# First gates and weight loads regrouped, and the attention bias added by VectorE instead of TensorE, in a hybrid decoder layer on eight cores

## The chip, the cores and the metric

The kernel runs on one Trainium2 chip, on all 8 of its cores. Each core works on one sequence of the batch and talks to no other. The time is the device time of the slowest core in microseconds (us), the median of several runs; lower is better. TensorE is called PE in the rows, VectorE DVE, ScalarE ACT, GpSimd POOL, and SP is the engine that issues most DMAs.

## What is computed

One decoder layer for x of 8 x 4096 x 1024, with two token mixers whose results are gated and merged, and an MLP:

```python
h = rmsnorm(x, norm1_w)
q, k, v, xr, yr, ga, gr = split(h @ w_in)          # 512, 512, 512, 1024 x4
# A: block-sparse attention, 8 heads of 64; q and k normed per head
s = (q @ k.T) * scale + bias_tab[bucket(q_pos - k_pos)]   # 32 buckets per head
# a query sees its own block of 256 keys (causal) and the 3 past blocks whose
# mean key scores best
A = softmax(s) @ v
# B: causal conv of width 4, then the gated linear recurrence
u = conv(xr);  a = exp(-8 * sigmoid(u @ Wa) * softplus(-lam))
hr = scan(a, sqrt(1 - a*a) * sigmoid(u @ Wi) * u)
B = hr * gelu(yr)
merged = sigmoid(ga) * (A @ w_proj_attn) + sigmoid(gr) * (B @ w_proj_rnn)
x = x + merged @ w_out
x = x + relu(rmsnorm(x) @ w_ff1)**2 @ w_ff2
```

## The kernel before

The program is recorded as a list of operations, and a list scheduler with a cost model of its own turns the list into one fixed order per engine. Each engine then works through its order and waits on semaphores. The order in which the code records work therefore sets priorities, and the scheduler may pull a later piece forward. Every engine instruction carries the line of the recorder (L475) and every DMA that of the DMA recorder (L480), so rows are told apart by their tile names.

The work of one core falls into three stages.

**Stage A, the front end.** The 4096 tokens are 32 tiles of 128. For a tile, `FEn` loads x (`xs`), norms it (`hb`, needing the norm weights `nw`), transposes it on PE and copies it to `hT`, which is also stored to `h_s` in HBM. `FEp` makes q and k and normalizes them per head, with short POOL, ACT and DVE steps (`ssq`, `qa`, `ktm`), and `FEv` makes v: 24 matmuls of 512 columns with `wqkv` per tile. Between the tiles the code records the recurrence of the first chunk: a chunk is 512 tokens, `RNN(0, ct)` stands at tiles 14, 16, ..., 28 for the eight column tiles ct, and `RNN2(0, g)` at tiles 21 and 29. `RNN` is 16 matmuls (`wx`, `wy`) and the convolution on DVE (`cv`), `RNN2` the two gates, the scan on DVE (`ii`) and the product `orn`.

**Stage B.** For chunks s = 1 to 7 the code records `RNN(s)`, `GATE1(s-1, m)` for the eight m, and `RNN2(s)`. `GATE1(c, m)` is 8 matmuls with `wga` (their tanh `t1` is stored to HBM as `t_s`), 8 with `wgr`, and 8 with `wpr` on `orn`; DVE multiplies the last two (`t2`, stored as `rm_s`).

**Stage C.** Attention for chunks c = 0 to 7 is cut into small units that are dealt out between dense units (gating, output projection, `W1`, `W2`) by a running `goal` and by `marks`, before which a chunk's attention must be recorded. During attention(0) the dense units are `GATE1(7, m)`. A unit of attention is one key tile of 128 keys of one head: a score matmul S into a PSUM bank (`qT`, `kTr`; banks 0 and 1, and bank 3 once `GATE1(7)` is done), the bias for the tiles that need one, an exp on ACT (`PT`) and up to four matmuls with V into an output bank (`Vr`). After the last tile of a head DVE takes a reciprocal (`rcp`) and scales the output (`otm`). The bias is a matmul of the identity with a table `BT`, added to the score bank; it covers 128 columns for the tile just before the chunk and 256, 256, 256 and 128 for the chunk's own four tiles. Gating loads `t1r` and `rmr` from HBM and combines them on DVE into `mT`.

Of the kernel before, what the change touches and what calls it, by code (L numbers as in the profile page):

```python
# [1297 lines left out]
```

How the kernel before makes its waits and increments, by code:

```python
        def run(ename, h):  # L282
            for i in order[ename]:
                for s, v in waits[i]:
                    h.wait_ge(sems[s], v)
                ins = ops[i].fn(h)
                if sig[i] is not None:
                    ins.then_inc(sems[sig[i][0]], 16 if ops[i].dsem is not None else 1)
            if ename == "sync":
                for s, v in fw.items():
                    h.wait_ge(sems[s], v)
```

## Time and profile before

| what | value |
| --- | --- |
| median of 3 runs | 2408.96 us (2406.88 to 2409.96) |
| the profiled execution, its own time | 2405.57 us |
| span of its slowest core, core 5 | 2404.0 us (the others 2392.4 to 2401.3) |
| PE busy | 2288.5 us, 95% |
| ACT busy | 1321.6 us, 55% |
| DVE busy | 1070.9 us, 45% |
| POOL busy | 612.6 us, 25% |
| mean granted TensorE clock, by core | 0.983 to 0.988 of full speed |

All rows are from the slowest core of that execution. Busy shares are averages over the three stages: the front end runs from 0 to about 210 us, stage B to about 830 us (the first score matmul starts at 832.6), and the rest is stage C. "PEclk" is the clock that was granted to TensorE as a share of full speed, so a stretch can lose time with PE idle or with PE slow.

### The profile page before, as it was taken

Reading aid. Unit: us, or ns where it says so; the run is one execution under the profiler, and the core shown is the slowest. Engines: PE = TensorE matmul, PEld = TensorE weight load, DVE = VectorE, ACT = ScalarE, POOL = GpSimd, SP = SyncE. Lnnn points to the kernel's source line nnn. Section 1 sums busy time; section 2 is a strip of 40 time slices with the busy share of each in tenths; the row PEclk is TensorE's granted clock in tenths of the full one; section 3 lists DMA queues with packets and bytes.
Section 4 is the critical chain, followed back from the end, with each engine's and each line's share of the span. In section 5 each row is a group of like instructions: output and inputs, shape, how many; then the busy total and the mean of one; then the engine's idle time right before and its main releaser. Section 6 shows DMA issues by size and latency. Waiting matters only on the chain.

```text
span 2404.0 us, 43880 instructions; the slowest of 8 cores (2392.4 to 2404.0 us)
## 1 busy us (share of the span) xinstructions
PE 2288.5 (95%) x14806; PEld 1127.5 (47%) x14806; DVE 1070.9 (45%) x1913; ACT 1321.6 (55%) x2341; POOL 612.6 (25%) x593
## 2 busy tenths in 40 slices
PE   3899989999999988999999999999999999999999
PEld 1444434444444444454555545555555455554444
DVE  2478777778778732423333332314222321232332
ACT  2568666676776735554636537554665375563111
POOL 3587753444444401101101001101100200110200
PEclk9899999999999988999999999999999999999999
DMA  6963665556562458256555565556455644644543
GB/s 148 236 192 135 147 141 117 114 121 143 123 136 72 126 168 238 96 167 168 166 166 165 181 162 182 144 172 192 139 169 169 189 142 152 178 159 135 173 166 123
DMA packets 194598, 373.47 MB, mean 155 GB/s; under 512 B 15507, under 2 KB 106684, under 8 KB 176316
## 3 DMA queue, kind: packets, MB, share of 16 engines
q1 hardware_dynamic: 188684, 336.04, 45.3%
q0 software_dynamic: 5696, 34.61, 9.5%
q8 instruction: 126, 2.06, 0.4%
q14 instruction: 92, 0.75, 0.1%
HBM read 332.30 MB, written 91.76 MB: 176 GB/s over the span
## 4 chain that ended last, share of the span: by engine, by line
PE 83%; DMA 5%; issue 4%; DVE 3%; POOL 2%; ACT 1%; SPq 1%; DVEq 0%; POOLq 0%; ACTq 0%
PE bank L475 83%; POOL s_ssq L475 2%; DMA s_xs<-x 1%; DMA s_t1r<-t_s 1%; DMA s_rmr<-rm_s 1%; SPq L480 1%; DMA k_s<-s_kst 1%; DMA rm_s<-s_t_0 1%; DMA s_wpr<-wpr_p 0%; DMA s_qT<-s_mskT 0%; DVE s_cv L475 0%; DVE s_ii L475 0%; DVE s_ssq L475 0%; DVE s_mT L475 0%; ACT L475 0%
## 5 line engine op out<-in xcount | busy, mean ns | idle before, releaser
L475 ACT ACTIVATE s_PT<-bank 128x512 bf16<-128x512 f32 (+3 forms) x1152 | 588.7, 564 | 315.1 <-PE bank L475 308.2
L475 PE MATMUL bank<-s_h2T,s_wsl 128*128 128x512 bf16 x2048 | 522.6, 380 | 3.2 <-DVE s_h2T L475 2.9
L475 PE MATMUL bank<-s_uT,s_wsl 128*128 128x512 bf16 x2048 | 513.0, 379 | 0.0
L475 PEld LDWEIGHTS bank<-s_Vr,s_PT 128*128 128x128 bf16 x4224 | 272.0, 98 | 257.0 <-issue 25.8
L475 PE MATMUL bank<-s_qT,s_kTr 80*128 80x512 bf16 (+3 forms) x1152 | 370.6, 364 | 4.9 <-DMA s_qT<-s_mskT 3.6
L475 ACT ACTIVATE s_rl<-bank 128x512 f32<-128x512 f32 x256 | 152.8, 597 | 320.3 <-PE bank L475 311.0
L475 PE MATMUL bank<-s_Vr,s_PT 128*128 128x65 bf16 x4224 | 314.0, 194 | 9.1 <-ACT s_PT L475 7.3
L475 DVE TENSOR_TENSOR s_uT<-s_rl 128x512 bf16<-128x512 f32 x176 | 122.6, 697 | 378.9 <-ACT s_rl L475 378.8
L475 PEld LDWEIGHTS bank<-s_h2T,s_wsl 128*128 128x128 bf16 x2048 | 189.4, 98 | 178.8 <-issue 7.7
L475 PEld LDWEIGHTS bank<-s_uT,s_wsl 128*128 128x128 bf16 x2048 | 182.5, 98 | 163.5 <-issue 2.9
L475 DVE TENSOR_TENSOR s_x1T<-bank,s_x1T 128x512 f32<-128x512 f32 x128 | 88.2, 689 | 365.2 <-PE bank L475 364.8
L475 POOL TENSOR_TENSOR s_uT<-s_rl 128x512 bf16<-128x512 f32 x80 | 83.9, 1048 | 608.6 <-ACT s_rl L475 559.9
L475 PE MATMUL bank<-s_wqkv,s_hT 128*128 128x512 bf16 x768 | 193.6, 396 | 13.5 <-ACT s_hT L475 9.0
L475 DVE SCALAR_TENSOR_TENSOR s_cv<-s_xr,s_pvec,s_cv 128x512 f32<-128x512 f32 x192 | 160.6, 896 | 1.0 <-ACT s_cv L475 0.3
L475 POOL TENSOR_TENSOR s_mT<-s_t1r,s_rmr 128x512 bf16<-128x512 f32 x32 | 40.8, 1274 | 440.9 <-DVE s_t1r L475 413.3
L475 PE MATMUL bank<-s_mT,s_wo 128*128 128x512 bf16 x512 | 131.2, 388 | 10.4 <-DVE s_mT L475 6.0
L475 POOL TENSOR_TENSOR s_orn<-s_ii,s_gq 128x512 bf16<-128x512 f32 x64 | 113.1, 1780 | 105.5 <-DVE s_ii L475 105.4
L475 POOL TENSOR_TENSOR s_ss<-s_ss,s_sqt 128x512 f32<-128x512 f32 x48 | 60.8, 1267 | 290.9 <-ACT s_sqt L475 289.7
L475 PEld LDWEIGHTS bank<-s_qT,s_kTr 80*128 80x128 bf16 x1152 | 108.8, 98 | 54.4 <-issue 8.6
L475 PE MATMUL bank<-s_orn,s_wpr 128*128 128x512 bf16 x512 | 125.1, 385 | 5.9 <-POOL s_orn L475 4.1
L475 PE MATMUL bank<-s_hTb,s_wga 128*128 128x512 bf16 x512 | 123.4, 382 | 5.3 <-ACT s_cv L475 5.3
L475 PE MATMUL bank<-s_hTb,s_wy 128*128 128x512 bf16 x512 | 122.7, 382 | 2.3 <-ACT s_gq L475 2.3
(120 smaller groups left out, 2728.8 us busy)
## 6 DMA issues: line engine op xcount, KB each, us to landing
s_wsl<-wff_s SPq DMA_DIRECT2D x128, 1024.0 KB, 6.0
s_xs<-x SPq DMA_DIRECT2D x32, 512.0 KB, 4.8
wff_s<-wff_p POOLq DMA_DIRECT2D x16, 1024.0 KB, 13.5
s_t1r<-t_s SPq DMA_DIRECT2D x64, 256.0 KB, 3.7
s_rmr<-rm_s SPq DMA_DIRECT2D x64, 256.0 KB, 4.3
s_x1T<-xT SPq DMA_DIRECT2D x64, 256.0 KB, 4.3
outT<-s_x1T SPq DMA_DIRECT2D x64, 256.0 KB, 5.3
h_s<-s_hT SPq DMA_DIRECT2D x32, 256.0 KB, 4.4
```

What stands on the lines that cost most here:

```text
L475: return P.add(eng, lambda e, m=meth, kw=kw: getattr(e, m)(**kw), reads, writes, cost=c_, lat=lat, fam=fam, tag=tag or (writes[0] if write ...
L480: return P.add(q, lambda e: e.dma_start(out=out, in_=in_), reads, writes, dsem=dsem, cost=(1000.0 if q == "gpsimd" else 80.0), nbytes=nb, ...
```

## The change

It has five parts. First, the bias is no longer a matmul: after S, DVE adds `BT` to the bank in place. Second, `GATE1` is cut in two: `GA(s, m)` with `wga` is recorded with chunk s itself, from s = 0 on, and `GR(s-1, m)` with `wgr` and `wpr` a chunk later, so that only `GR(7, m)` is left for attention(0). Third, `RNN(0)` and `RNN2(0)` leave the front end: column tiles 0 to 3 stand at tiles 28 to 31, the rest in `stageB(0)`. Fourth, the first loads stand in another order and wait for one another, `xs` has 4 buffers and `hT` 6, and the weights of the recurrence are loaded at every second tile. Fifth, `wpa` and `wo` are loaded before attention(0) instead of during it, for which SBUF is laid out anew.

```diff
         load_x(0)
+        dma("sync", nw, nw_d, "c0b", [], ["nw"])
         dma("sync", identb, cid_d, "c0a", [], ["identb"])
-        dma("sync", nw, nw_d, "c0b", [], ["nw"])
-        load_x(1)
...
-        load_x(2)
...
+        for t in range(1, NXS):
+            load_x(t, P.after("nw") if t == 1 else P.after("xs%d" % (t - 1)))
...
-            if wB:
+            if t % 2 == 0 and wB:
                 w_, src, nm = wB.pop(0)
...
-            if t >= 14 and t % 2 == 0 and t < 30:
-                RNN(0, [(t - 14) // 2], rbank)
-            if t == 21:
-                RNN2(0, 0, rbank)
-            if t == 29:
-                RNN2(0, 1, rbank)
+            if t >= 28:
+                RNN(0, [t - 28], rbank)
...
-        def GATE1(c, m, bank):
-            hk = ["hTb%d" % (c % NHB)]
+        def GA(c, m, bank):
...
+            for dt_ in range(8):
+                op("tensor", "matmul", ["hTb%d" % (c % NHB), "wga%d" % p], ["B%d" % b], tag="gate", out=bankf[b], lhsT=wga[p][:, dt_, o_:o_ + 128], rhs=h_[:, :, dt_, :],
+                   start=(dt_ == 0), stop=(dt_ == 7))
+            op("scalar", "activation", ["B%d" % b, "hbias"], ["t1_%d" % s], out=t1[s], in_=bankf[b], func=AF.Tanh, scale=0.5, bias=hbias[:, m, 2:3])
+            dma("sync", t1_s[c, m], t1[s], "t1_%d" % s, ["t1_%d" % s], ["t1_s%d_%d" % (c, m)])
+
+        def GR(c, m, bank):
...
         def stageB(s, g, between=None):
-            RNN(s, range(NR * g, NR * g + NR), dbank)
+            if s + g > 0:
+                RNN(s, range(NR * g, NR * g + NR), dbank)
...
+            for half in range(2):
+                for m in range(4 * g + 2 * half, 4 * g + 2 * half + 2):
+                    GA(s, m, dbank)
+                    if s > 0:
+                        GR(s - 1, m, dbank)
+                if half == 0:
+                    if between is not None:
+                        between()
+                    RNN2(s, g, dbank)
...
-        for s in range(1, NCH):
+        for s in range(NCH):
...
-                           lhsT=kTr[ks][0:80, hi * nk * 128 + kt * 128:hi * nk * 128 + (kt + 1) * 128], rhs=qT[s][0:80, h, q0:CH], start=True, stop=bias is None)
+                           lhsT=kTr[ks][0:80, hi * nk * 128 + kt * 128:hi * nk * 128 + (kt + 1) * 128], rhs=qT[s][0:80, h, q0:CH], start=True, stop=True)
                         if bias is not None:
                             qb, b0, nb_ = bias
-                            op("tensor", "matmul", ["BT", "identb"], ["B%d" % sb], tag="S", out=bankf[sb][:, qb - q0:qb - q0 + nb_], lhsT=identb,
-                               rhs=BT[:, h, b0:b0 + nb_], start=False, stop=True)
+                            sl_ = bankf[sb][:, qb - q0:qb - q0 + nb_]
+                            op("vector", "tensor_tensor", ["B%d" % sb, "BT"], ["B%d" % sb], tag="bias", out=sl_, in0=sl_, in1=BT[:, h, b0:b0 + nb_], op=ALU.add)
...
         def early():
+            dma("sync", wpa, wpo[:, 0:4, :], "wpa", ["wpo_s0"], ["wpa"])
+            for i in range(2):
+                dma("sync", wo[:, 4 * i:4 * i + 4, :], wpo[:, 4 + 4 * i:8 + 4 * i, :], "wo", ["wpo_s1"], ["wo:%d" % i])
...
-                GATE1(NCH - 1, m, gbank7)
...
+                GR(NCH - 1, m, gbank7)
...
-        extend([(5200.0, gate1u(m)) for m in range(8)])
...
+        for m in range(8):
+            extend([(3460.0, gate1u(m))])
+            if m == 5:
+                marks[0] = len(dense)
+            if m > 5:
+                extend(g0[2 * m - 12:2 * m - 10])
```

What the scheduler makes of it is seen in each engine's order. The first place is the start of SP's order, with the loads of x (`xs`), the norm weights (`nw`) and the small constants; first before, then after the change, with the semaphores waited for.

```order
L480 DMA s_xs0<-x 128x1024
L480 DMA s_identb<-c_identb 128x128
L480 DMA s_nw<-nw_bc 128x1024
L480 DMA s_xs1<-x 128x1024
L480 DMA s_xs2<-x 128x1024
L480 DMA s_pvec<-pvec 128x88
```

```order
L480 DMA s_xs0<-x 128x1024
L480 DMA s_nw<-nw_bc 128x1024
L480 DMA s_identb<-c_identb 128x128
L480 DMA s_qkcol<-qk_col 128x2
L480 DMA s_pvec<-pvec 128x88
L480 DMA s_nwc<-nw_col 128x8
L480 DMA s_mtab<-c_mtab 128x768
L480 DMA s_cv0<-c_G 33x384
L480 DMA s_ii0<-rel_bias 32x8 [waits e_vector]
L480 DMA s_xs1<-x 128x1024 [waits d_c0b]
```

The second x tile (`xs1`) has moved from the fourth place to the tenth, behind all the constants, and waits for `nw` (semaphore c0b) to land.

The second place is PE's order near the end of attention(0), whose heads have four key tiles (S of 512, 384, 256 and 128 columns). `s_hTb,s_wgr` and `s_orn,s_wpr` are what is left of the gates, `s_Vr,s_PT` the matmuls with V. First before, from the last pieces of the gates on:

```order
L475 MATMUL bank<-s_hTb,s_wgr 128x512
L475 MATMUL bank<-s_orn,s_wpr 128x512 x8
L475 MATMUL bank<-s_qT,s_kTr 128x256
L475 MATMUL bank<-s_BT,s_identb 128x256
L475 MATMUL bank<-s_Vr,s_PT 128x65
L475 MATMUL bank<-s_qT,s_kTr 128x384
L475 MATMUL bank<-s_BT,s_identb 128x256
L475 MATMUL bank<-s_Vr,s_PT 128x65 x4
```

And after:

```order
L475 MATMUL bank<-s_orn,s_wpr 128x512
L475 MATMUL bank<-s_Vr,s_PT 128x65
L475 MATMUL bank<-s_kmBD,s_qp 128x32 x4
L475 MATMUL bank<-s_identb,s_maskb 128x128
L475 MATMUL bank<-s_kmBD,s_qp 128x32 x4
L475 MATMUL bank<-s_identb,s_maskb 128x128
L475 MATMUL bank<-s_qT,s_kTr 128x512
L475 MATMUL bank<-s_identb,s_maskb 128x128
L475 MATMUL bank<-s_Vr,s_PT 128x65 x4
L475 MATMUL bank<-s_qT,s_kTr 128x256
L475 MATMUL bank<-s_qT,s_kTr 128x384
```

Before, the last gate matmuls stand ahead of the last two heads; now they stand ahead of the last four, and behind them PE has only scores and V matmuls until the transposes at the end of attention(0). One gate unit is left for attention(1).

The third place is DVE's order at the start of attention(1), with gating(0) beside it; bank0 and bank1 are score banks, `d_t1r0` and `d_rmr1` wait for DMAs. Before:

```order
L475 SCALAR_TENSOR_TENSOR s_t1r0<-s_t1r0,bank5 128x512 [waits e_tensor,d_t1r0]
L475 SCALAR_TENSOR_TENSOR s_t1r1<-s_t1r1,bank6 128x512 [waits e_tensor,d_t1r1]
L475 TENSOR_TENSOR s_mT<-s_t1r1,s_rmr1 128x512 [waits e_vector,d_rmr1]
L475 RECIPROCAL s_rcp<-bank2 128x4 [waits e_tensor]
L475 TENSOR_TENSOR s_otm<-bank2,s_rcp 128x4x64 [waits e_vector]
L475 SCALAR_TENSOR_TENSOR s_t1r0<-s_t1r0,bank7 128x512 [waits d_t1r0]
```

And after:

```order
L475 SCALAR_TENSOR_TENSOR s_t1r0<-s_t1r0,bank5 128x512 [waits e_tensor,d_t1r0]
L475 TENSOR_TENSOR bank1<-bank1,s_BT 128x128 [waits e_tensor]
L475 SCALAR_TENSOR_TENSOR s_t1r1<-s_t1r1,bank6 128x512 [waits e_tensor,d_t1r1]
L475 TENSOR_TENSOR bank0<-bank0,s_BT 128x256 [waits e_tensor]
L475 TENSOR_TENSOR s_mT<-s_t1r1,s_rmr1 128x512 [waits e_vector,d_rmr1]
L475 TENSOR_TENSOR bank1<-bank1,s_BT 128x256 [waits e_tensor]
L475 TENSOR_TENSOR bank0<-bank0,s_BT 128x256 [waits e_tensor]
L475 TENSOR_TENSOR bank1<-bank1,s_BT 128x128 [waits e_tensor]
```

The five adds of a head now stand among gating's instructions on the same engine, some right behind one that waits for a load.

## Rows read from the trace of the kernel before

**Rows 1.** Page, busy time by engine (PE matmuls, PEld weight loads).

```profile
PE 2288.5 (95%) x14806; PEld 1127.5 (47%) x14806; DVE 1070.9 (45%) x1913; ACT 1321.6 (55%) x2341; POOL 612.6 (25%) x593
```

**Rows 2.** Windows: length, busy us (instructions) per engine, PEclk, DMA share, GB/s.

```profile
0.00:60.00 60.00, 23.09 (x110) 10.18 (x111) 16.53 (x39) 16.52 (x27) 22.33 (x32) 0.93 0.62 147
60.00:120.00 60.00, 52.40 (x285) 25.00 (x284) 28.44 (x42) 32.94 (x53) 31.04 (x41) 0.87 0.92 236
120.00:340.00 220.00, 199.26 (x1157) 97.55 (x1155) 172.84 (x270) 146.53 (x232) 157.63 (x179) 0.98 0.59 158
340.00:840.00 500.00, 494.13 (x2277) 222.45 (x2276) 383.33 (x540) 350.06 (x529) 211.69 (x180) 1.00 0.52 119
840.00:900.00 60.00, 52.14 (x335) 26.79 (x334) 21.23 (x63) 21.42 (x46) 4.71 (x3) 0.90 0.50 168
900.00:950.00 50.00, 38.72 (x347) 19.98 (x346) 12.85 (x28) 29.06 (x63) 5.05 (x4) 0.88 1.01 270
950.00:1120.00 170.00, 159.77 (x1117) 80.28 (x1115) 64.22 (x183) 80.62 (x155) 26.21 (x23) 0.95 0.48 142
1120.00:2340.00 1220.00, 1208.40 (x8912) 617.94 (x8910) 356.95 (x732) 634.88 (x1223) 148.77 (x129) 1.00 0.54 164
2340.00:2404.00 64.00, 60.61 (x281) 27.30 (x279) 14.52 (x21) 9.55 (x16) 5.20 (x5) 0.99 0.36 132
```

**Rows 3.** Timeline of PE in attention beside the MLP: start, us, instruction, count.

```profile
1608.73 0.60 PE L475 MATMUL bank<-s_qT,s_kTr 80*128 80x512 bf16 x2
1609.16 0.22 PE L475 MATMUL bank<-s_BT,s_identb 128*128 128x128 bf16 x1
1609.22 0.38 PE L475 MATMUL bank<-s_qT,s_kTr 80*128 80x512 bf16 x1
1609.44 0.27 PE L475 MATMUL bank<-s_BT,s_identb 128*128 128x256 bf16 x1
1609.55 1.02 PE L475 MATMUL bank<-s_uT,s_wsl 128*128 128x512 bf16 x4
```

**Rows 4.** Groups by form on PE: busy us, mean ns | idle before, releaser.

```profile
L475 PE MATMUL bank<-s_BT,s_identb 128*128 128x256 bf16 x192 | 51.3, 274 | 0.0
L475 PE MATMUL bank<-s_BT,s_identb 128*128 128x128 bf16 x120 | 26.5, 222 | 0.0
```

**Rows 5.** Groups by form on DVE, 900 to 2340 us, same columns.

```profile
L475 DVE SCALAR_TENSOR_TENSOR s_t1r<-s_t1r,bank 128x512 f32<-128x512 f32 x64 | 43.8, 685 | 66.3 <-PE bank L475 46.4 <-DMA s_t1r<-t_s 18.8
...
L475 DVE TENSOR_TENSOR s_otm<-bank,s_rcp 128x256 bf16<-128x256 f32 x56 | 23.7, 424 | 5.3
...
L475 DVE TENSOR_TENSOR s_gm<-bank,s_mtab 128x128 f32<-128x128 f32 x24 | 6.8, 283 | 0.4 <-PE bank L475 0.3
```

**Rows 6.** Timeline of the start, all engines; in brackets the idle before.

```profile
16.73 1.28 DVE L475 SCALAR_TENSOR_TENSOR s_hb<-s_xs,s_rstd,s_nw 128x1024 bf16<-128x1024 f32 x1 [14.88 <-DMA s_nw<-nw_bc]
...
24.70 1.06 ACT L475 ACTIVATE s_junk<-s_xs 128x1024 bf16<-128x1024 f32 x1 [17.54 <-DMA s_xs<-x]
...
26.99 3.57 PE L475 MATMUL bank<-s_wqkv,s_hT 128*128 128x512 bf16 x8 [7.71 <-ACT s_hT L475]
...
36.88 4.36 PE L475 MATMUL bank<-s_wqkv,s_hT 128*128 128x512 bf16 x10
```

**Rows 7.** Chain that ended last, 0 to 340 us: start, us, what.

```profile
73.71 15.45 DMA k_s<-s_kst
```

**Rows 8.** Waits of PE, 200 to 345 us: us in total, times, longest.

```profile
PE bank L475 <- ACT s_cv L475: 5.3, 1, 5.3
PE bank L475 <- ACT s_hT L475: 3.9, 1, 3.9
```

**Rows 9.** Timeline of DVE at the end of attention(0), two heads' ends.

```profile
892.63 0.18 DVE L475 RECIPROCAL s_rcp<-bank 128x4 f32<-128x4 f32 x1 [1.02 <-PE bank L475]
...
895.10 0.18 DVE L475 RECIPROCAL s_rcp<-bank 128x4 f32<-128x4 f32 x1 [1.75 <-PE bank L475]
```

**Rows 10.** Waits of DVE, 840 to 960 us: us in total, times, longest.

```profile
DVE s_t1r L475 <- DMA s_t1r<-t_s: 12.9, 5, 4.1
```

More of the change, by code:

```diff
@@ L539, in build_nc @@
         pA_peak = cur[0]
+        orn, wga, wgr, wpr = [], [], [], []
         tok_tiles = x_d.rearrange("(n p) d -> n p d", p=128)
@@ L778, in build_nc @@
         st.append(contextlib.ExitStack())
-        for i in range(2, NHB):
-            hTb[i] = alloc("hTb%d" % i, [TPC, 8, 128], BF16)
-        wga, wgr, wpr = [], [], []
+        orn += [alloc("orn%d" % i, [CH], BF16) for i in range(8)]
+        baseC = cur[0]
+        hTb[2] = alloc("hTb2", [TPC, 8, 128], BF16)
         for p in range(4):
@@ L798, in GATE1 @@
             sos = [(c * 8 + i) % NORN for i in range(8)]
-            for j, (w_, wk, dst, dk) in enumerate(((wga[p], "wga%d" % p, t1[s], "t1_%d" % s), (wgr[p], "wgr%d" % p, t2[s], "t2_%d" % s))):
-                b = bank()
-                for dt_ in range(8):
-                    op("tensor", "matmul", hk + [wk], ["B%d" % b], tag="gate", out=bankf[b], lhsT=w_[:, dt_, o_:o_ + 128], rhs=h_[:, :, dt_, :],
-                       start=(dt_ == 0), stop=(dt_ == 7))
-                op("scalar", "activation", ["B%d" % b, "hbias"], [dk], out=dst, in_=bankf[b], func=AF.Tanh, scale=0.5, bias=hbias[:, m, 2 + j:3 + j])
-            dma("sync", t1_s[c, m], t1[s], "t1_%d" % s, ["t1_%d" % s], ["t1_s%d_%d" % (c, m)])
+            b = bank()
+            for dt_ in range(8):
+                op("tensor", "matmul", ["hTb%d" % (c % NHB), "wgr%d" % p], ["B%d" % b], tag="gate", out=bankf[b], lhsT=wgr[p][:, dt_, o_:o_ + 128], rhs=h_[:, :, dt_, :],
+                   start=(dt_ == 0), stop=(dt_ == 7))
+            op("scalar", "activation", ["B%d" % b, "hbias"], ["t2_%d" % s], out=t2[s], in_=bankf[b], func=AF.Tanh, scale=0.5, bias=hbias[:, m, 3:4])
             b = bank()
@@ L822, in build_nc @@
             dma("gpsimd", wga[p], wr_d[2, p].rearrange("p (a b) -> p a b", a=8), "wga%d" % p, [], ["wga%d" % p])
+        for p in range(4):
             dma("gpsimd", wgr[p], wr_d[3, p].rearrange("p (a b) -> p a b", a=8), "wgr%d" % p, [], ["wgr%d" % p])
@@ L856, in build_nc @@
         st.append(contextlib.ExitStack())
-        kTr = [alloc("kTr%d" % i, [S], BF16) for i in range(2)]
-        qT = [alloc("qT%d" % i, [NH, CH], BF16) for i in range(2)]
-        qp = alloc("qp", [4, CH], BF16)
+        kTr = [alloc("kTr0", [S], BF16)]
+        wpa = alloc("wpa", [4, D], BF16)
+        wo = alloc("wo", [8, D], BF16)
+        sqt = [alloc("sqt%d" % i, [CH], F32) for i in range(2)]
         alloc("gap", [16], F32)
-        Vr = [alloc("Vr%d" % i, [NCH * VW], BF16) for i in range(2)]
+        qT = [alloc("qT0", [NH, CH], BF16)]
+        Vr = [alloc("Vr0", [NCH * VW], BF16)]
         gm = alloc("gm", [NH, 16], F32)
@@ L869, in build_nc @@
         rcp = alloc("rcp", [4], F32)
-        otm = alloc("otm", [4, 512], BF16)
         assert cur[0] <= endX, (cur[0], endX)
+        kTr.append(alloc("kTr1", [S], BF16))
+        qT.append(alloc("qT1", [NH, CH], BF16))
+        qp = alloc("qp", [4, CH], BF16)
+        Vr.append(alloc("Vr1", [NCH * VW], BF16))
         NPT = 6
         PT = [alloc("PT%d" % i, [CH], BF16) for i in range(NPT)]
-        oT = [alloc("oT%d" % i, [4, CH], BF16) for i in range(2)]
-        wpa = alloc("wpa", [4, D], BF16)
-        wo = alloc("wo", [8, D], BF16)
-        t1r = [alloc("t1r%d" % i, [CH], F32) for i in range(2)]
+        otm = alloc("otm", [4, 512], BF16)
+        oT = [alloc("oT0", [4, CH], BF16)]
+        ss = alloc("ss", [CH], F32)
+        rs2 = alloc("rs2", [CH], F32)
+        t1r = [alloc("t1r0", [CH], F32)]
+        assert cur[0] <= endR, (cur[0], endR)
+        if endR - cur[0] > 64:
+            alloc("gap2", [(endR - cur[0]) // 64 * 32], BF16)
+        mT = alloc("mT", [8, CH], BF16)
+        oT.append(alloc("oT1", [4, CH], BF16))
+        NRL = 2
+        rl = [alloc("rl%d" % i, [CH], F32) for i in range(NRL)]
+        t1r.append(alloc("t1r1", [CH], F32))
         rmr = [alloc("rmr%d" % i, [CH], F32) for i in range(2)]
+        assert cur[0] <= baseC, (cur[0], baseC)
         uT = alloc("uT", [16, CH], BF16)
```

69 lines of the change are left out of this document (29 added, 40 removed).

## Prediction

> **What bounds the kernel now.** I read the busy times first: TensorE is busy for 95% of the span, no other engine for more than 55% [rows 1]. So the questions are where matmul time goes away and where TensorE idles or runs slow. The windows answer the second: of each stretch take the length less the PE busy time, and add the length times what PEclk lacks of 1. From 0 to 60 us that is 36.9 idle + 4.2 of clock, 60 to 120: 7.6 + 7.8, 120 to 340: 20.7 + 4.4, so 82 us lost before 340. Stage B, 340 to 840, loses 5.9 in all. From 840 to 1120, with attention(0), attention(1) and the first gating and MLP, it is 7.9 + 6.0, 11.3 + 6.0 and 10.2 + 8.5, so 50 us. From 1120 to 2340 TensorE loses 11.6 us of 1220 [rows 2]. The kernel is thus TensorE-bound where most of the attention runs, and has two weak places, the start and the hand-over to attention, which the regrouping touches.
>
> **The bias.** The identity matmuls last 274 and 222 ns in the groups [rows 4], but the engine pipelines, so the price is the spacing of starts: the 128-column one starts at 1609.16 and the next matmul at 1609.22, 0.06 us; the 256-column one holds 1609.44 to 1609.55, 0.11 us [rows 3]. All 192 and 120 of them make 192 x 0.11 + 120 x 0.06 = 28.3 us. They are worth this only where TensorE is the bound. Chunks 2 to 7 lie there: 48 heads of three 256s and two 128s, 48 x (0.33 + 0.12) = 21.6 us. Attention(0) and (1) run where TensorE idles, and I count nothing for them. **Term: -21.6**, bounds -28.3 and, were the slots idle, 0.
>
> The 128-column price can be set against a page. The row says 0.06 us. The Trainium skill, "TensorE: Matmul & The Clock Gate", section "Back-to-back issue gap", gives a sustained spacing of about 81 ns for 128 columns; by it the 120 narrow ones would be worth 9.7 us instead of 7.2, and the sum would be 2.5 us lower. The row is of this very matmul, so I keep it.
>
> On VectorE the trace has no such add. The nearest rows with one PSUM operand: `otm` with 256 columns 424 ns, `gm` with 128 columns and a float result 283 ns [rows 5]. That is 192 x 0.424 + 120 x 0.283 = 115 us more on an engine that is busy 357 of 1220 us in the long stretch [rows 2], so its own time is covered by matmuls. What can be exposed is latency: S, add, exp and the V matmuls of a tile follow one another, and the score bank is held 0.3 to 0.4 us longer. With dense matmuls as filler this costs little: the exp already stands in that chain, and the 11.6 us lost in the stretch are all that it and everything else cost. Bounds: 0 (all covered) and 115 (each add exposed). It is nearest to the covered row, so I take **+3**.
>
> **The start.** Now the first `hb` waits 14.9 us for `nw` and begins at 16.73; the second x tile lands at 24.70, when ACT begins on it [rows 6]. After the change `nw` is second and comes sooner, but x1 leaves only once `nw` is there and still shares the DMA engines with `wqkv`, so tile 1 will hardly be earlier than 24. What can be gained is that q, k and v of tile 0 run in between: its first 8 matmuls start at 26.99, the next ones only at 36.88 [rows 6]. As DVE and POOL are what the front end's later tiles wait for, I take -3 (bounds 0 and -12, the gap between those two blocks plus what `nw` brings).
>
> **Front end and first stage of B.** Without the weights of the recurrence at every tile and with RNN(0) later, DMA is less crowded between 40 and 120 us: it is 92% busy there, and the chain has one link of 15.45 us, a store of k [rows 2, 7]. I take -8 (bounds 0 and -15.4, all that 60 to 120 loses). Against this stands that nothing is saved on DVE: RNN(0) takes as much wherever it stands. Stage B spends 383 of 500 us on DVE [rows 2]; a chunk there has 336 matmuls of 512 columns at 0.215 us (two S take 1608.73 to 1609.16 [rows 3]), 72 us, and so 55 us of DVE. The new stage 0 has some 230 matmuls, 50 us, for the same 55 us: DVE becomes its limit, for about 5 us. The hand-over now has waits of 5.3 and 3.9 us [rows 8], which GA(0) can fill as it needs no recurrence. I take -4 for this part, stall included (bounds +5 and -9.2). **Term for 0 to 340: -15**, bounds +5 and -37.
>
> **Hand-over to attention.** GA(7), 64 matmuls of 0.215 = 13.8 us, moves from attention(0) into stage B. That is no gain in itself: matmuls are moved, and attention(0) loses their cover. By the order, four heads instead of two now run bare. A bare head takes 895.10 - 892.63 = 2.5 us from one reciprocal to the next [rows 9], of which S, bias and V matmuls fill about 1; with four adds of 0.28 to 0.42 over two banks I make it 3.3, idle 2.4. So 4 x 2.4 - 2 x 1.5 = +6.6. In attention(1) the adds lengthen a head's chain by about as much as the matmuls shorten TensorE's list, +1. In return the two `wo` loads and the `wpa` load are out of the way when DMA is at 1.01 [rows 2], and DVE's 12.9 us of waiting for `t1r` [rows 10] should shrink; I take -8 from a bound of -12.9. The last gates beside gating(0) fill a bubble, -4. That sums to -4.4. **Term: -4**, bounds +10 and -15.
>
> **Sum:** -21.6 + 3 - 15 - 4 = -37.6. On the profiled execution's 2405.6 this gives 2368.0. The median stands 3.4 above that execution, so I forecast **2371 us**, 1.6% faster. That, give or take 15, is the first case: 2356 to 2385.
>
> **Rivals.** *A, VectorE's line becomes the bound (slower).* The adds stand in DVE's fixed order between instructions that wait: 18.8 us for `t1r` [rows 5], most of it in attention(1) [rows 10], and the new order puts adds right behind those. While one waits, the add, the exp and the V matmuls wait too, and TensorE behind them. For: the order itself, and a whole-chain exposure of 115 us. Against: in the long stretch DVE is 29% busy, and with the adds about 37%. It decides from the point where some 38 us more than my 3 are exposed, a third of 115. At half of the 115, 57 us, the time is 2409 - 38 + 54 = 2425. The Trainium skill, "PSUM — Partial Sum Buffer", section "Engine vs sequencer instructions", says that VectorE's queue is strictly first in, first out, so nothing overtakes the waiting instruction; no row yet shows adds behind one.
>
> *B, the regrouping gives nothing.* The front end is held by short DVE and POOL steps, which stay, DVE takes over stage 0, and the barer heads eat what the DMAs give. Only the bias remains: 2409 - 21.6 + 3 = 2390, range 2385 to 2404. For: DVE at 79% and POOL at 72% from 120 to 340 [rows 2].
>
> *C, all of it pays.* Both weak places reach near their lower bounds, -30 and -12: 2409 - 21.6 - 42 = 2345, range 2325 to 2355. For: the 82 and 50 us lost there. Against: the regrouping leaves the longest DVE and POOL chains as they are.
>
> *D, the freed slots are idle slots.* If TensorE merely waits elsewhere once the bias matmuls are gone and the regrouping nets nothing, the time stays at 2409. Against: the identity matmuls start right on the spacing of their neighbours [rows 3], with no idle before them [rows 4].
>
> **How the numbers follow.** First case 0.50, B 0.22, C 0.11, D 0.06, A 0.11. The prediction is the first. Range 2336 to 2404: it reaches through B above and into most of C below, leaving out A, D and the low end of C, about 0.2. A measurement of this kernel can tell about 0.2% from no change, 5 us. Faster by more: first, B and C, 0.83. Same: D, 0.06. Slower: A, 0.11.
>
> **What would show it.** Right: no identity matmuls with `BT` on PE, and 312 adds near 424 and 283 ns on DVE; 1120 to 2340's work some 21 us shorter with PE still near 99% busy; the start to the first gates of stage B about 15 us shorter; `t1r` waits below 12.9. Wrong: PE waits for `PT` that were not there, growing in step with DVE's waits on DMA or on PE; adds far from 0.4 us; a front end as long as before; bare heads of attention(0) well over 3.3 us; or a lower granted clock where heads run bare, which would cost again as much as the idling.

## The result and the profile after

The changed kernel takes 2395.51 us in the median (2392.58 for its profiled execution, the lowest of its runs), against 2409.46 for the kernel before on the same chip. The ratio is 0.994, with a 95% interval of 0.992 to 0.9959: faster by 0.6%, where 1.6% was forecast. In the profiled execution of one experiment below (e1) one die was disturbed, so its rows are from a core of the other die.

The busy times by engine [rows 1 before]:

```profile
PE 2267.0 (95%) x14494; PEld 1105.3 (46%) x14494; DVE 1171.3 (49%) x2225; ACT 1333.0 (56%) x2345; POOL 612.7 (26%) x593
```

312 matmuls are gone from PE, and 312 instructions have come to DVE. The adds, in the groups by form, are close to the rows that priced them [rows 5]:

```profile
L475 DVE TENSOR_TENSOR bank<-bank,s_BT 128x256 f32<-128x256 f32 x192 | 79.3, 428 | 74.9 <-PE bank L475 73.8
L475 DVE TENSOR_TENSOR bank<-bank,s_BT 128x128 f32<-128x128 f32 x120 | 35.5, 296 | 76.0 <-PE bank L475 75.9
```

The windows of the same stretches, of core 6, the slowest [rows 2]:

```profile
0.00:60.00 60.00, 17.62 (x63) 7.02 (x64) 9.26 (x28) 11.92 (x19) 11.89 (x20) 0.91 0.61 140
60.00:120.00 60.00, 53.22 (x311) 26.84 (x310) 37.46 (x54) 36.24 (x60) 40.44 (x56) 0.90 0.82 222
120.00:340.00 220.00, 207.00 (x1202) 101.65 (x1201) 159.20 (x245) 150.49 (x233) 150.74 (x171) 0.99 0.66 173
340.00:840.00 500.00, 490.02 (x2255) 220.07 (x2253) 385.84 (x547) 347.00 (x524) 212.47 (x180) 1.00 0.53 118
840.00:900.00 60.00, 45.20 (x249) 20.99 (x247) 35.95 (x94) 24.06 (x46) 11.38 (x8) 0.85 0.45 134
900.00:950.00 50.00, 38.37 (x270) 18.45 (x270) 24.64 (x65) 25.49 (x54) 3.80 (x3) 0.70 0.80 230
1120.00:2340.00 1220.00, 1209.88 (x8835) 610.58 (x8834) 422.85 (x938) 647.21 (x1239) 151.97 (x131) 1.00 0.54 166
```

The long stretch is as full as before (1209.88 of 1220 busy) although DVE has 66 us more to do in it. The front end from 60 to 340 is fuller, the first 60 us are emptier, and the hand-over from 840 to 950 is worse, in idle time and in granted clock.

Windows at fixed times hold different work in the two kernels. Milestones do not. The groups by tile show the first and the last start of an instruction (count, shortest/median/longest ns, first to last start us); the first score matmul (`s_kTr`) ends stage B, and the first matmul on `s_h2T` starts the first MLP. Before:

```profile
L475 PE MATMUL bank<-s_qT,s_kTr x1152: 219/380/631, 832.6 to 2194.8; 80*128 80x512 bf16 x175, 80*128 80x256 bf16 x11, 80*128 80x384 bf16 x4, 80*128 80x128 bf16 x2
L475 PE MATMUL bank<-s_h2T,s_wsl x2048: 376/379/634, 971.7 to 2372.6; 128*128 128x512 bf16 x187
```

After:

```profile
L475 PE MATMUL bank<-s_qT,s_kTr x1152: 217/380/631, 845.6 to 2179.1; 80*128 80x512 bf16 x172, 80*128 80x256 bf16 x13, 80*128 80x384 bf16 x5, 80*128 80x128 bf16 x2
L475 PE MATMUL bank<-s_h2T,s_wsl x2048: 376/379/634, 981.0 to 2359.4; 128*128 128x512 bf16 x187
```

GA(7), 64 matmuls, now lies before the first of these milestones. The table takes it out of either side at the 13.8 us of the prediction:

| stretch | before | after | moved by GA(7) | difference | forecast |
| --- | --- | --- | --- | --- | --- |
| start to first score | 832.6 | 845.6 | -13.8 | -0.8 | -15 |
| first score to first `h2T` | 139.1 | 135.4 | +13.8 | +10.1 | -4 |
| first to last `h2T` | 1400.9 | 1378.4 | 0 | -22.5 | -21.6 + 3 |
| last `h2T` to the end of the span | 31.4 | 31.3 | 0 | -0.1 | 0 |

They add up to the 13.3 us between the spans. The bias did what was forecast, and a little more. Both terms of the regrouping missed, by 14 us each.

Two cautions. The table is of the slowest core of each run, and the cores of one run differ: the second stretch takes 134.9 to 141.0 us on the eight cores before and 131.3 to 137.2 after. The medians of the eight cores give much the same differences, -2.5, +10.3 and -24.9. And the 13.8 us assume that GA(7) costs its full length in either place. The run e9 below shows that it does not, so of the first two rows only their sum is firm: +9.3, where -19 was forecast.

### The profile page after: what moved, and what is told of

Same layout as the page of the kernel before. It is cut to its first block, busy times and chain, and to the rows that moved or that the text cites. A ratio compares the mean times of both kernels' runs of the same rounds, so it can differ in the third digit from the quotient of the medians.

```text
span 2390.7 us, 43783 instructions; the slowest of 8 cores (2374.7 to 2390.7 us)
## 1 busy us (share of the span) xinstructions
PE 2267.0 (95%) x14494; PEld 1105.3 (46%) x14494; DVE 1171.3 (49%) x2225; ACT 1333.0 (56%) x2345; POOL 612.7 (26%) x593
## 3 DMA queue, kind: packets, MB, share of 16 engines
q0 software_dynamic: 5696, 34.61, 10.1%
## 4 chain that ended last, share of the span: by engine, by line
PE 84%; DMA 5%; issue 4%; DVE 3%; POOL 2%; ACT 1%; SPq 0%; DVEq 0%; POOLq 0%; ACTq 0%
PE bank L475 84%; POOL s_ssq L475 1%; DMA s_pvec<-pvec 1%; DMA s_t1r<-t_s 1%; DMA s_xs<-x 1%; DMA rm_s<-s_t_0 1%; DMA s_qT<-s_mskT 1%; DMA outT<-s_x1T 1%; DVE s_cv L475 0%; SPq L480 0%; DVE s_ii L475 0%; DMA s_x1T<-xT 0%; ACT s_PT L475 0%; DVE s_ssq L475 0%; DVE s_t1r L475 0%
## 5 line engine op out<-in xcount | busy, mean ns | idle before, releaser
L475 PE MATMUL bank<-s_uT,s_wsl 128*128 128x512 bf16 x2048 | 518.9, 379 | 1.5 <-DVE s_mskT L475 0.9
L475 PE MATMUL bank<-s_h2T,s_wsl 128*128 128x512 bf16 x2048 | 516.8, 380 | 0.8 <-DVE s_h2T L475 0.8
L475 PE MATMUL bank<-s_qT,s_kTr 80*128 80x512 bf16 (+3 forms) x1152 | 376.0, 370 | 9.2 <-ACT s_PT L475 4.0
L475 PE MATMUL bank<-s_Vr,s_PT 128*128 128x65 bf16 x4224 | 315.5, 195 | 12.1 <-ACT s_PT L475 11.7
L475 PE MATMUL bank<-s_wqkv,s_hT 128*128 128x512 bf16 x768 | 191.5, 396 | 21.2 <-ACT s_hT L475 16.4
L475 DVE TENSOR_TENSOR bank<-bank,s_BT 128x256 f32<-128x256 f32 (+1 forms) x312 | 111.3, 378 | 150.9 <-PE bank L475 149.7
L475 PEld LDWEIGHTS bank<-s_qT,s_kTr 80*128 80x128 bf16 x1152 | 108.7, 99 | 54.9 <-issue 16.5
L475 PE MATMUL bank<-s_hTb,s_wgr 128*128 128x512 bf16 x512 | 124.2, 383 | 3.5 <-ACT s_t_0 L475 2.0
```

What stands on the lines that cost most here:

```text
L475: return P.add(eng, lambda e, m=meth, kw=kw: getattr(e, m)(**kw), reads, writes, cost=c_, lat=lat, fam=fam, tag=tag or (writes[0] if write ...
```

## The experiments

Each time is given as a ratio to the kernel before, run beside it on the same chip (its 95% interval in brackets). The changed kernel was run again, on the chip of e15, e11 and e6, and gave 0.993 (0.9917 to 0.9944); with the first 0.994 that makes two marks to compare with. Ratios from different chips are compared with more care.

> The changed kernel once more, beside the next three on one chip: 0.992 to 0.996 of the kernel before.

**The parts apart.** The first run puts the identity matmul back into the changed kernel, the second puts the add alone into the kernel before.

```diff
 # e1_matmul_bias, on the changed kernel
-                            op("vector", "tensor_tensor", ["B%d" % sb, "BT"], ["B%d" % sb], tag="bias", out=sl_, in0=sl_, in1=BT[:, h, b0:b0 + nb_], op=ALU.add)
+                            op("tensor", "matmul", ["BT", "identb"], ["B%d" % sb], tag="S", out=bankf[sb][:, qb - q0:qb - q0 + nb_], lhsT=identb,
+                               rhs=BT[:, h, b0:b0 + nb_], start=False, stop=True)
...
 # e2_add_alone, on the kernel before: the same lines with + and - exchanged
```

> The changed kernel with the bias as identity matmuls again: the regrouping alone. Theory T1 (the adds save 21 us where TensorE is the bound and cost some 10 in attention(0) and attention(1); the regrouping nets about nothing because its start is later): 2403 to 2411 us. Rival T2 (the regrouping gains the forecast 15 to 20 us and the adds give nothing back): 2388 to 2395 us.

> The kernel before with the bias added by VectorE, nothing regrouped. T1: 2409 - 21, plus 1.4 us for each of two bare heads of attention(0) and about 4 us in attention(1), so 2391 to 2397 us. T2 (the adds' latency eats what the matmuls free): 2405 us or more.

Measured: the regrouping alone 1.0003 (0.9982 to 1.0023), the add alone 0.9913 (0.9889 to 0.9937). T1 holds: the whole gain is the bias, and the regrouping is worth nothing (e2 came out some 3 us faster than T1's 2391 to 2397). The milestones say the same: with the add alone the scores start at 838.8, `h2T` at 982.3, and it ends at 2363.4, so 143.5 and 1381.1 us against 139.1 and 1400.9.

```profile
L475 PE MATMUL bank<-s_qT,s_kTr x1152: 217/380/634, 838.8 to 2183.0; 80*128 80x512 bf16 x172, 80*128 80x256 bf16 x12, 80*128 80x384 bf16 x4, 80*128 80x128 bf16 x4
L475 PE MATMUL bank<-s_h2T,s_wsl x2048: 376/379/634, 982.3 to 2363.4; 128*128 128x512 bf16 x187
```

For the regrouping alone, on core 3, the hand-over takes 976.4 - 843.8 = 132.6 us and the long stretch 1396.9:

```profile
L475 PE MATMUL bank<-s_qT,s_kTr x1152: 216/379/631, 843.8 to 2194.7; 80*128 80x512 bf16 x172, 80*128 80x256 bf16 x13, 80*128 80x384 bf16 x4, 80*128 80x128 bf16 x3
L475 PE MATMUL bank<-s_h2T,s_wsl x2048: 376/379/634, 976.4 to 2373.3; 128*128 128x512 bf16 x187
```

So on these cores the add costs the hand-over 4.4 us (143.5 - 139.1), the regrouping 7.3 (132.6 + 13.8 - 139.1), and together they make 11.7, near the 10.1 measured. By the medians of the cores (for e1 of cores 0 to 3) it is 2.1 and 5.7, so the split holds to about 2 us. The 7.3 rests on the 13.8 us of GA(7).

**The start.** The timeline of the changed kernel shows two things that the prediction did not see:

```profile
8.92 1.28 DVE L475 SCALAR_TENSOR_TENSOR s_hb<-s_xs,s_rstd,s_nw 128x1024 bf16<-128x1024 f32 x1 [7.07 <-POOL s_rstd L475]
16.38 1.01 PE L475 MATMUL bank<-s_identb,s_hb 128*128 128x128 bf16 x8 [16.38 <-DMA s_identb<-c_identb]
...
28.86 0.22 ACT L475 ACTIVATE s_tmp<-s_pvec 128x8 f32<-128x8 f32 x1 [21.25 <-DMA s_pvec<-pvec]
...
29.29 0.99 ACT L475 COPY s_hT<-bank 128x1024 bf16<-128x1024 bf16 x1
...
30.53 3.57 PE L475 MATMUL bank<-s_wqkv,s_hT 128*128 128x512 bf16 x8 [13.15 <-ACT s_hT L475]
```

`hb` is ready at 10.2, 8 us sooner than before [rows 6], but the identity, now behind `nw`, lands at 16.4; and the copy of `hT`, ready from 17.4, runs at 29.29, because on ACT it stands behind an exp of `pvec`, which waits 21.25 us for its load. The code records that exp at tile 6; the scheduler hoisted it to the place right behind the first tile's square.

The kernel before has the same fault in a milder form. Its first copy stands on ACT behind the square of the second x tile, the row at 24.70 of [rows 6], which waits for that tile to land:

```profile
25.75 0.99 ACT L475 COPY s_hT<-bank 128x1024 bf16<-128x1024 bf16 x1
```

```diff
 # e15_pvec_late
-                dma("sync", pvec, pvec_d.rearrange("p (t j) -> p t j", t=8, j=11), "c0c", [], ["pvec"])
+                dma("sync", pvec, pvec_d.rearrange("p (t j) -> p t j", t=8, j=11), "c0c", [], ["pvec"], extra=P.after("hT%d" % (5 % NHT)))
 # e5_start: the same, and
+        dma("sync", identb, cid_d, "c0a", [], ["identb"])
         dma("sync", nw, nw_d, "c0b", [], ["nw"])
-        dma("sync", identb, cid_d, "c0a", [], ["identb"])
 # e17_unchained: e15_pvec_late, and
-            load_x(t, P.after("nw") if t == 1 else P.after("xs%d" % (t - 1)))
+            load_x(t)
```

> The changed kernel with the identity loaded ahead of nw again and the load of pvec held back until the sixth tile has been transposed. T1 (the first copy of hT stands behind an exp that waits for pvec until 28.9 us, and the first transpose waits for the identity until 16.4): the first q matmul starts near 22 instead of 30.5 and 6 to 11 us are gained, 2384 to 2390 us. Rival (wqkv or the second x tile sets the time, or stage 0 gives it back): 2393 to 2398 us.

> The changed kernel with one edit: the load of pvec waits for the sixth tile's hT, nw stays ahead of the identity. T1 (the exp that waits for pvec in ACT's line is what holds the first tile; the identity's place does not matter, since wqkv lands only near 21 us): the first q matmul near 21 us instead of 30.5, and as much gained as with the identity ahead too, 0.6 to 0.9% under the changed kernel. Rival (the identity's wait is half of it): under 0.4%.

> pvec late as in e15_pvec_late, and the first x loads no longer wait for one another or for nw. If the chaining delays the second tile for nothing: x1 lands before 28 us instead of 31.6 and 2 to 5 us are gained on e15_pvec_late. If the chaining protects wqkv and the identity: the first transpose comes after 18 us, and it is 0 to 4 us slower.

Measured: e5_start 0.9868 (0.9838 to 0.9898), e15_pvec_late 0.9886 (0.9868 to 0.9904), e17_unchained 0.9855 (0.9834 to 0.9876). Holding `pvec` back, that one edit, gains 0.44% on the changed kernel beside it, 10.6 us. That lies between T1's 0.6 to 0.9% and the rival's 0.4%. The copy no longer waits, as T1 says, and the first q matmul starts at 18.65, sooner than the 21 expected:

```profile
16.28 1.01 PE L475 MATMUL bank<-s_identb,s_hb 128*128 128x128 bf16 x8 [16.28 <-DMA s_identb<-c_identb]
17.39 1.01 ACT L475 COPY s_hT<-bank 128x1024 bf16<-128x1024 bf16 x1 [9.54 <-PE bank L475]
...
18.65 3.57 PE L475 MATMUL bank<-s_wqkv,s_hT 128*128 128x512 bf16 x8 [1.35 <-ACT s_hT L475]
```

The identity still lands at 16.3. With it ahead as well (e5_start) the ratio is 0.18% lower, on another chip and with overlapping intervals, so what its place is worth can't be told. As a whole e5_start gained 0.6 to 0.7%, 15 to 17 us, more than its T1 had. The chaining of the x loads may cost something: with it the second tile's square starts at 31.57, without it at 23.77, and the ratio goes from 0.9886 to 0.9855. The intervals overlap, and the two were on different chips, so that step, some 7 us, is likely rather than shown.

e17_unchained also warns against reading too much into the first q matmul. There the copy stands behind the square of the second tile again, and the first q matmul starts at 26.07, as late as in the kernel before:

```profile
23.77 1.06 ACT L475 ACTIVATE s_junk<-s_xs 128x1024 bf16<-128x1024 f32 x1 [16.67 <-DMA s_xs<-x]
24.83 0.99 ACT L475 COPY s_hT<-bank 128x1024 bf16<-128x1024 bf16 x1
26.07 2.72 PE L475 MATMUL bank<-s_wqkv,s_hT 128*128 128x512 bf16 x6 [9.11 <-ACT s_hT L475]
```

Yet by the windows TensorE is busy for 29.45 of the first 60 us, against 25.51 in e15_pvec_late and 17.62 in the changed kernel. So the load of `pvec` is what cost the time, but a first matmul that starts soon is not what the gain follows: what the first 60 us get done is nearer to it.

**Where the front end's gain goes.** The changed kernel's front end is faster once it runs: its last matmul with `wqkv` starts at 276.5 instead of 321.9 (not at about 210, as the section on the profile before has it), without RNN(0). But from there to the 64th `wpr` matmul, near 400, the windows show TensorE idling again:

```profile
84.00:276.00 192.00, 183.96 (x1153) 94.14 (x1151) 138.56 (x219) 118.90 (x191) 142.75 (x172) 0.99 0.74 200
276.00:400.00 124.00, 113.91 (x520) 50.08 (x519) 88.67 (x130) 97.34 (x143) 57.77 (x51) 0.99 0.39 99
```

10 of 124 us are idle where before it was 2.1 of 65 (62.90 busy from 322 to 387). DVE is busy 88.67 of 124, 72%, so it is not the limit that the prediction named.

```diff
 # e16_rnn0_early
-            if t >= 28:
-                RNN(0, [t - 28], rbank)
+            if t >= 22 and t % 2 == 0 and t < 30:
+                RNN(0, [(t - 22) // 2], rbank)
```

> The changed kernel with the first four column tiles of RNN(0) recorded at tiles 22, 24, 26 and 28 instead of 28 to 31. If stage 0 loses its 12 us because the recurrence of chunk 0 starts too late: 3 to 8 us gained, the front end ending a little later and the first wpr matmuls earlier. If the chain of the recurrence itself holds stage 0 (DVE and ACT steps in turn), or the front end gives it back: within 3 us of the changed kernel.

Measured 0.9939 (0.9917 to 0.996), no change: the recurrence's late start is not the cause. That its chain of DVE and ACT steps holds stage 0 fits, but is argued, not shown.

**The hand-over.** Where the bare heads run, the reciprocals of DVE stand 3.9 us apart, against 2.5 before [rows 9] and 3.3 forecast:

```profile
895.95 0.17 DVE L475 RECIPROCAL s_rcp<-bank 128x4 f32<-128x4 f32 x1
...
899.87 0.17 DVE L475 RECIPROCAL s_rcp<-bank 128x4 f32<-128x4 f32 x1
```

Not all of this is the add. With the regrouping alone (e1, core 3), where the bias is a matmul, the bare heads stand 3.2 us apart:

```profile
898.07 0.18 DVE L475 RECIPROCAL s_rcp<-bank 128x4 f32<-128x4 f32 x1 [2.48 <-PE bank L475]
...
901.25 0.18 DVE L475 RECIPROCAL s_rcp<-bank 128x4 f32<-128x4 f32 x1 [2.47 <-PE bank L475]
```

What the add does there shows in TensorE's waits for the exp (`PT`), 840 to 960 us, in this order: before, after, the regrouping alone (e1, core 3), the add alone (e2).

```profile
PE bank L475 <- ACT s_PT L475: 4.5, 12, 0.7
PE bank L475 <- ACT s_PT L475: 12.3, 23, 1.3
PE bank L475 <- ACT s_PT L475: 5.0, 14, 0.5
PE bank L475 <- ACT s_PT L475: 13.7, 22, 1.8
```

These waits are one of the signs by which the prediction said it would be wrong, and they come with the add alone.

The granted clock is lower too: from 900 to 950 PEclk is 0.70, where it was 0.88. Over the whole of 840 to 1120, before and after:

```profile
840.00:1120.00 280.00, 250.63 (x1795) 127.05 (x1794) 98.30 (x274) 131.09 (x263) 35.98 (x30) 0.93 0.58 170
```

```profile
840.00:1120.00 280.00, 241.80 (x1617) 117.81 (x1616) 145.02 (x400) 132.99 (x260) 41.00 (x34) 0.88 0.56 164
```

Idle rises from 29.4 to 38.2 us, the clock's share from 0.07 x 280 = 19.6 to 0.12 x 280 = 33.6. The clock's share counts idle time as well, in which a low clock costs nothing, so it is an upper bound. Which runs have the lower clock is clear. Those that keep identity matmuls in chunks 0 and 1 (before, e1, e3, e6, e18, e20) have 0.92 or 0.93 in this window, those that have none there (after, e2, e7, e8, e9, e11, e15, e16, e17) 0.86 to 0.90. What it costs is not: e7, without any bias, has 0.88 as well, and its hand-over is among the shortest.

DVE's waits for `t1r`, 12.9 us before [rows 10], have all but gone after the change. It was not the moved loads that did it. In order: after, the regrouping alone (e1, core 3), the add alone (e2).

```profile
DVE s_t1r L475 <- DMA s_t1r<-t_s: 1.1, 2, 0.6
DVE s_t1r L475 <- DMA s_t1r<-t_s: 13.5, 4, 6.9
DVE s_t1r L475 <- DMA s_t1r<-t_s: 2.6, 2, 1.4
```

With `wo` and `wpa` loaded early and no adds, DVE waits as long as before; with the adds and those loads where they were, it hardly waits. All eight cores of e2 say the same (at most 2.8 us). So the wait shrank with the adds, not with the loads. That DVE has the adds to do while the data comes in fits this, and then the shorter wait is no gain.

Four edits take the hand-over apart. The first keeps matmuls for the chunks of the hand-over, the second leaves the bias out, the third keeps GA(7) as filler in attention(0), the fourth deals attention(0) out over all eight gate units and records gating(0) behind it.

```diff
 # e3_matmul_first_two: identity matmul if c < 2, else the add
+                        if bias is not None and (c < 2):
...
+                        elif bias is not None:
 # e7_no_bias: neither
 # e9_ga7_filler
-                    GA(s, m, dbank)
+                    if s < NCH - 1:
+                        GA(s, m, dbank)
...
+                GA(NCH - 1, m, gbank7)
                 GR(NCH - 1, m, gbank7)
...
-            extend([(3460.0, gate1u(m))])
+            extend([(5200.0, gate1u(m))])
 # e11_pace
-            if m == 5:
-                marks[0] = len(dense)
-            if m > 5:
-                extend(g0[2 * m - 12:2 * m - 10])
-        extend(g0[4:5])
+        marks[0] = len(dense)
+        extend(g0[0:5])
...
-            goal = tot0 * (i + 1) / 6 if i < 5 else ...
+            goal = tot0 * (i + 1) / 9 if i < 8 else ...
```

> The changed kernel with identity matmuls for chunks 0 and 1 only, adds for chunks 2 to 7. T1 (in the bare heads the add lengthens the chain from 2.5 to 3.9 us a head): 8 to 12 us under the changed kernel, 2384 to 2388 us. Rival (the hand-over is slow for lack of filler alone, the add does not matter): 2394 to 2398 us.

> The changed kernel with no bias at all, neither matmul nor add (the scores lack it). What it is faster than the changed kernel by is all that the 312 adds cost. T1 (the adds are covered from chunk 2 on and cost in the hand-over, mostly by TensorE's lower clock): 8 to 14 us under the changed kernel, nearly all of it between 840 and 960 us. Rival (they cost everywhere, in step with their number): over 20 us, spread over the long stretch. Third way (the bare heads cost the same without them): under 4 us.

> The changed kernel with GA(7) kept out of stage B and done with GR(7) during attention(0), 64 matmuls of filler more there. If missing filler is what the hand-over lost: 4 to 10 us under the changed kernel. If the heads at the end stay bare anyway (its order has four of them) and only the add and the granted clock count: within 3 us of it.

> The changed kernel with attention(0) dealt out over all eight gate units, a ninth to each, and gating(0) recorded behind it. If the hand-over is slow because the units are dealt too fast for the filler, 5 to 10 us are gained; if the scheduler hoists the gates ahead of the heads whatever the recording says, four or five heads stay bare and the time stays within 4 us of the changed kernel. I expect the second.

Measured: e3 0.9904 (0.988 to 0.9929), e7 0.9901 (0.9862 to 0.994), e9 0.9931 (0.9912 to 0.995), e11 0.9917 (0.9904 to 0.9931). e7 bounds what the adds cost in all: it lies 0.29% under 0.993 and 0.39% under 0.994, so 7 to 9 us, at the lower end of T1's 8 to 14, with a wide interval. Its milestones, 842.3 and 972.0, put 135.4 - 129.7 = 5.7 us of that into the hand-over, where matmuls (e3) take 131.8. Its long stretch takes 2351.1 - 972.0 = 1379.1 us, against 1378.4 with the adds: there they cost nothing. In time e3's gain does not stand clear of the intervals (0.26 to 0.36%, on another chip than either mark).

```profile
L475 PE MATMUL bank<-s_qT,s_kTr x1152: 216/380/634, 842.3 to 2172.1; 80*128 80x512 bf16 x173, 80*128 80x256 bf16 x13, 80*128 80x384 bf16 x4, 80*128 80x128 bf16 x2
L475 PE MATMUL bank<-s_h2T,s_wsl x2048: 376/379/631, 972.0 to 2351.1; 128*128 128x512 bf16 x187
```

e9 is the instructive miss. Its milestones:

```profile
L475 PE MATMUL bank<-s_qT,s_kTr x1152: 216/380/634, 841.6 to 2182.5; 80*128 80x512 bf16 x173, 80*128 80x256 bf16 x13, 80*128 80x128 bf16 x3, 80*128 80x384 bf16 x3
L475 PE MATMUL bank<-s_h2T,s_wsl x1967: 376/379/634, 984.0 to 2360.0; 128*128 128x512 bf16 x197
```

Of GA(7)'s 64 matmuls 56 now start behind the first score, while 7 more with `wgr` start ahead of it (windows by tile), so 49 matmuls, 10.5 us, have changed sides. The hand-over is as fast as the filler theory wants: 984.0 - 841.6 = 142.4, less 10.5 makes 131.9 instead of 135.4, and by the medians of the cores 128.1 instead of 135.2. But the scores start only 4.0 us sooner than in the changed kernel, though 10.5 us of matmuls have left stage B, and by the medians, 841.5 in both, no sooner at all. So GA(7) fills gaps wherever it stands, and its move is worth nothing. It also means that the table above charges the hand-over too much, and the start too little, by taking GA(7) at 13.8 us.

e11 lies within the noise in time, as expected (0.13% under the changed kernel on the same chip), and its heads still run bare: the reciprocals of core 1 stand 3.4 to 3.9 us apart from 890 to 901. But its hand-over is shorter, 131.7 us in the median of the cores (128.7 to 134.6) against 135.2 (134.2 to 136.9) for the changed kernel on that chip. So the order of gates and gating(0) is worth some 3 us there, which the time alone does not show.

**The long stretch.** To see whether the adds are covered there, they were doubled:

```diff
 # e8_double_add
                             op("vector", "tensor_tensor", ["B%d" % sb, "BT"], ["B%d" % sb], tag="bias", out=sl_, in0=sl_, in1=BT[:, h, b0:b0 + nb_], op=ALU.add)
+                            if c >= 2:
+                                op("vector", "tensor_tensor", ["B%d" % sb, "BT"], ["B%d" % sb], tag="bias", out=sl_, in0=sl_, in1=BT[:, h, b0:b0 + nb_], op=ALU.add)
```

> The changed kernel with every add of chunks 2 to 7 made twice, so that the bias counts double there (the output is not the reference's): 240 more adds on VectorE, 93 us at the durations measured, and each such tile's chain longer by 0.3 to 0.4 us. T1 (adds are covered where dense matmuls fill TensorE): 0 to 5 us over the changed kernel. Rival A of the prediction (VectorE's line is what waits): 15 us or more over it, and the waits of PE for PT grow.

Measured 0.9952 (0.9935 to 0.9969), 0.1 to 0.2% or 3 to 5 us over the changed kernel. VectorE is busy for 1245.1 us instead of 1171.3, 74 us more. Rival A is out in the long stretch, and e7's 7 to 9 us for all the adds put it out as a whole.

```profile
1120.00:2340.00 1220.00, 1209.03 (x8827) 610.01 (x8826) 485.89 (x1146) 649.83 (x1238) 150.93 (x131) 1.00 0.54 165
```

With DVE at 486 instead of 423 us PE is as busy as ever, and waits for `PT` for 2.0 us in this stretch, against 2.9 in the kernel before.

**Together.** The edits that helped were combined: e6 is e5_start with e3, e18 is e15 with e3, e20 is e17 with e3.

> The identity and pvec as in e5_start, and identity matmuls as the bias of chunks 0 and 1 as in e3_matmul_first_two. T1 (the two losses are independent): the sum of both gains, 20 to 26 us under the changed kernel. Rival (the earlier start is taken back at the hand-over, or the matmuls there gain nothing): no more than e5_start alone, 14 to 18 us.

> pvec late as in e15_pvec_late and identity matmuls for chunks 0 and 1 as in e3_matmul_first_two; nw stays ahead of the identity. T1: the first gives 10 us and the second 4, so 0.986 to 0.988 of the kernel before, the fastest of all so far or level with e6_both.

> The three edits that gained, together: pvec late, x loads not chained (e17_unchained), identity matmuls for chunks 0 and 1. If they add up: 0.981 to 0.984 of the kernel before. If the earlier start is taken back later: level with e17_unchained and e18_best at 0.985.

Measured: e6 0.9876 (0.9859 to 0.9892), e18 0.9851 (0.9826 to 0.9875), e20 0.9839 (0.9796 to 0.9883). e6 fell short of the sum and gained no more than e5_start; e18 came out a little better than expected. e18 and e20 beat both kernels, and the best estimate, 1.6% under the kernel before, is the gain that was forecast for the change. e20's interval covers e18 and e17, so which of them is fastest stays open. In e20 the clock from 900 to 950 stays at 0.97, though its attention starts 15 us sooner, so that this window holds later work than in the changed kernel:

```profile
900.00:950.00 50.00, 41.61 (x343) 20.71 (x346) 15.71 (x31) 29.92 (x63) 9.68 (x8) 0.97 0.75 235
```

## Why the prediction was wrong

**The bias, right.** The stretch with the bulk of the bias became 22.5 us shorter, against -21.6 + 3. Prices by spacing of starts were right, and so was the choice of the covered row for the adds: without them (e7) the stretch is no shorter, and doubling them cost 3 to 5 us for 74 us of VectorE. Rival D is out with it. Two slips in the working change nothing: the aside on the 128-column price takes all 120 narrow matmuls where the term counts 96, so it would move the sum by 2.0 us and not 2.5, and the 92% of DMA is of 60 to 120 us, not of 40 to 120.

**The start, wrong.** The step that failed is the -3: it rested on SP's order and on when x1 lands, and counted tile 0's matmuls as running meanwhile. They could not, since ACT's order has an exp that waits for `pvec` ahead of the first copy of `hT`. TensorE's wait between the first tile's transposes and its first q matmul was not 8 us but 13, and in the first 60 us TensorE was busy for 17.62 us, where it had been busy for 23.09 [rows 2]. The prediction had a row of the same kind before it and did not read it so: before, the copy waits on ACT behind the square of x1 [rows 6]. Holding that one load of `pvec` back gives 10.6 us.

With it held back the scores start at 831.9:

```profile
L475 PE MATMUL bank<-s_qT,s_kTr x1152: 217/380/634, 831.9 to 2167.0; 80*128 80x512 bf16 x172, 80*128 80x256 bf16 x13, 80*128 80x384 bf16 x5, 80*128 80x128 bf16 x2
```

Less GA(7)'s 13.8 that is 818.1, 14.5 us before the 832.6 of the kernel before, which looks like the forecast's -15. It is in part luck. The first q matmul starts 8.3 us sooner than before, where -3 stood, so the rest of the front end and the first stage of B brought 6 of the 12 forecast; and by e9 the 13.8 is too much.

The Trainium skill, "PSUM — Partial Sum Buffer", section "Engine vs sequencer instructions", says that ScalarE's queue too is strictly first in, first out; the copy that was ready at 17.4 and ran at 29.3 agrees. The prediction used that rule for VectorE alone.

**The hand-over, wrong.** -4 was forecast, +10.1 came by the table. The -8 for the moved loads failed: with the regrouping alone `t1r`'s waits stay at 13.5 us, and they fall to 1.1 only with the adds. The -4 for gates beside gating(0) failed too: e11 takes them away from there and its hand-over is some 3 us shorter. The bare heads cost 3.9 us, not 3.3, and here the base was off rather than the add: in the new order they take 3.2 with matmuls, not 2.5, and the add brings about 0.7, where 0.8 was forecast. By the runs (e2, e3, e7) the adds make 2 to 6 us of the loss, seen as TensorE's waits for `PT`. The regrouping's 6 to 7 us come with GA(7) at 13.8 us: e9 shows that its matmuls had been filling gaps, so that moving them away saved the hand-over less than that, and e11 gets back some 3 us by its order. What is left of it is not settled. The lower granted clock, which the prediction named as a danger, is there, and comes with the identity matmuls' going; e7 has it too and is no slower for it, so its price stays open.

**The first stage of B.** It gives back 8 us, 10 of idling in place of 2, where 5 were forecast, and not by DVE's load. What holds it is open.

Together: 37.6 us were forecast and 14 came. Holding `pvec` back returns 10.6 of the difference, and matmuls for chunks 0 and 1 on top of that (e18) make it 36 us; the last step is between runs on two chips whose intervals overlap.

The measured time is that of rival B, only the bias remaining, and not by its mechanism: it had the front end bound as before, while here a faster front end was paid for by a late start.

## What to carry to other kernels

When a scheduler orders the engines, read every engine's first rows for waits on loads, not only the queue that the edit names: a small constant needed late can stand ahead of the first copy. A wait that shrinks is not yet a gain: it can shrink because the one who waits comes later, so run the parts of a change apart before one of them gets the credit. In this kernel a matmul that merely adds a table was worth replacing by a VectorE add where dense matmuls cover the longer chain; where short chains run bare, the matmul was likely the better of the two. Work that fills gaps has no fixed price: moving GA(7) saved less than its length where it had stood and cost less where it went.
